# Prompt attention in a hybrid decoder layer: 64-row score tiles without key padding, scores two units ahead, softmax division on GpSimd

## What is computed

```python
A_HEADS = 16; A_KV = 4; A_HD = 64; A_GROUP = 4; WINDOW = 128; SEQ = 1024

def sink_attend(q, k, v, mask, sinks):
    s = jnp.einsum('...kgqd,...ksd->...kgqs', q, k).astype(f32) * (A_HD ** -0.5)
    s = jnp.where(mask, s, -jnp.inf)
    sk = sinks.astype(f32)[:, :, None]
    mx = jnp.maximum(jnp.max(s, axis=-1), sk)
    p = jnp.exp(s - mx[..., None])
    den = jnp.sum(p, axis=-1) + jnp.exp(sk - mx)
    return jnp.einsum('...kgqs,...ksd->...kgqd', (p / den[..., None]).astype(v.dtype), v)

def swa_prompt(q, k, v, sinks):
    # blocks of 128 queries read their own block of keys and the previous one
    ...
    mask = (diff >= 0) & (diff < WINDOW) & (kpos[:, None, :] >= 0)
    o = sink_attend(qb, band(k), band(v), mask[:, None, None], sinks)
```

## Time and profile before

| what | us |
|---|---|
| median of 3 runs | 1845.52 (1844.2 to 1847.49) |
| span of the profiled execution | 1838.2 |
| of it first half of the prompt attention | 549 to 677 |
| sampled tokens | 677 to 782 |
| second half of the prompt attention | 782 to 899 |
| busy in the whole span: PE | 1774.4 (97%) |
| DVE | 809.4 (44%) |
| ACT | 523.1 (28%) |
| POOL | 72.4 (4%) |

### The profile page before, as it was taken

One profiled execution on the slowest core, in us unless ns is written; L12 is line 12 of the kernel. 1 busy time (PEld: TensorE's weight loads), 2 busy tenths in 40 slices (PEclk: granted clock), 3 DMA queues, 4 the chain that ended last, 5 costly groups with the idle time before them and its releaser, 6 DMA issues.

```text
span 1838.2 us, 26328 instructions
## 1 busy us (share of the span) xinstructions
PE 1774.4 (97%) x10443; PEld 1622.1 (88%) x10443; DVE 809.4 (44%) x1769; ACT 523.1 (28%) x1191; POOL 72.4 (4%) x149
## 2 busy tenths in 40 slices
PE   7999977998999999999999999999999999999998
PEld 7999956996899888888999998888888889999996
DVE  5313212342115544466452544444444544444447
ACT  5424311331224533345330331211121222222222
POOL 3001110110100000000000100000000000000001
PEclk9999986998899999999999999999999999999999
DMA  6131125212512112311133011111111111111112
GB/s 199 48 90 43 45 60 94 41 35 73 72 29 41 24 32 50 67 24 24 24 93 109 24 47 47 46 46 46 46 46 40 30 44 46 46 46 46 46 58 97
DMA packets 140605, 99.26 MB, mean 54 GB/s; under 512 B 82328, under 2 KB 132512, under 8 KB 140520
## 3 DMA queue, kind: packets, MB, share of 16 engines
q1 hardware_dynamic: 140520, 98.08, 20.6%
HBM read 88.43 MB, written 11.60 MB: 54 GB/s over the span
## 4 chain that ended last, share of the span: by engine, by line
PE 85%; DMA 5%; SPq 1%; DVE 1%; ACT 0%; issue 0%; POOL 0%; POOLq 0%; ACTq 0%; DVEq 0%
PE bank L725 25%; PE bank L1077 21%; PE bank L1050 21%; PE bank L1036 6%; DMA out<-Cin 4%; PE bank L865 3%; PE bank L687 3%; PE bank L897 2%; PE bank L782 1%; PE bank L790 1%; PE bank L808 1%; PE bank L819 1%; PE bank L785 1%; DMA bc<-gate_rows 1%; DMA Cin<-in_state_n 0%; PE bank L765 0%
## 5 line engine op out<-in xcount | busy, mean ns | idle before, releaser
L1891 DVE TENSOR_TENSOR x<-bank,x 128x512 f32<-128x512 f32 x288 | 195.5, 689 | 139.2 <-PE bank L1077 137.5
L1050 PE MATMUL bank<-xT_hi,w_hi 128*128 128x384 f32 (+1 forms) x768 | 250.5, 326 | 1.0 <-DVE xT_lo L1513 1.0
L1050 PE MATMUL bank<-xT_hi,w_lo 128*128 128x384 f32 (+1 forms) x768 | 250.4, 326 | 0.0
L1050 PE MATMUL bank<-xT_lo,w_hi 128*128 128x384 f32 (+1 forms) x768 | 250.3, 326 | 0.0
L1077 PE MATMUL bank<-w_hi,hid_hi 128*128 128x512 f32 x576 | 227.1, 394 | 0.0
L1077 PE MATMUL bank<-w_lo,hid_hi 128*128 128x512 f32 x576 | 226.1, 392 | 0.0
L1077 PE MATMUL bank<-w_hi,hid_lo 128*128 128x512 f32 x512 | 204.1, 399 | 0.0
L725 PE MATMUL bank<-xT_hi,w_hi 128*128 128x384 f32 (+1 forms) x1008 | 197.7, 338 | 3.5 <-ACT w_hi L1124 3.5
L725 PE MATMUL bank<-xT_lo,w_hi 128*128 128x384 f32 (+1 forms) x1008 | 189.6, 330 | 0.0
L725 PE MATMUL bank<-xT_hi,w_lo 128*128 128x384 f32 (+1 forms) x1008 | 186.5, 326 | 0.0
L1448 ACT ACTIVATE relu<-bank 128x384 f32<-128x384 f32 (+1 forms) x96 | 45.4, 473 | 493.8 <-PE bank L1050 493.8
(11 more groups left out here) (204 smaller groups left out, 2330.8 us busy)
## 6 DMA issues: line engine op xcount, KB each, us to landing
raw<-in_w_in SPq DMA_DIRECT2D x64, 256.0 KB, 4.4
raw<-in_w_up SPq DMA_DIRECT2D x16, 1024.0 KB, 5.5
raw<-in_w_down SPq DMA_DIRECT2D x16, 1024.0 KB, 4.9
raw<-in_w_in SPq DMA_DIRECT2D x10, 1024.0 KB, 5.9
xin<-in_x_prompt SPq DMA_DIRECT2D x8, 512.0 KB, 4.0
Cin<-in_state_C SPq DMA_DIRECT2D x8, 512.0 KB, 4.4
bc<-gate_rows SPq DMA_DIRECT2D x32, 128.0 KB, 4.2
out<-Cin SPq DMA_DIRECT2D x8, 512.0 KB, 6.2
```

The source lines that it names most:

```text
L1050: last = nc.tensor.matmul(bank[n % 4][:, 0:cn], w[:, slot, k * WCOLS + tile * P:k * WCOLS + (tile + 1) * P], x[:, k, c0:c0 + cn], start=(s ...
L1891: nc.vector.tensor_tensor(v, bank[4 + d % 4][:, :], v, ALU.add).then_inc(free_v, 1)
```

## The change

Four things change together, all in the prompt attention.

First, the keys are kept without padding in `akT`, two heads in 128 rows. A score matmul takes 64 rows, rows 0 to 63 or 64 to 127, and they alternate; the two halves write different banks. To make that possible a unit is now a block with two query heads of each of two key heads (`gg`). ACT writes `akT` with one copy instead of two, GpSimd no longer clears `akz`, and the keys are transposed for the output with 4 transposes instead of 8 float32 matmuls. The value matmuls take columns from both units of the pair and run key block by key block.

Second, PE makes scores two units ahead: S(0) and S(1) before the first fill, S(n+2) in slot n. S(n+2) still waits for the mask of n+1, since banks 3 and 4 are as before. `prob` and `ast` have three buffers. ACT's order in a slot stays as it was.

Third, in the last slot of a half the transposes come before the fill.

Fourth, the division moves from DVE to GpSimd, with a power of -1 in place of the reciprocal.

```diff
-            akz = a("akz", [P, NKV, T])
+            akT = a("akT", [P, 2, T])
...
-                prob = a2("prob", [P, 2, GRP, 2 * P])
+                prob = a2("prob", [P, 3, GRP, 2 * P])
                 pT = a2("pT", [P, 2, 2, GRP * P])
-                ast = a2("ast", [P, 2, 6, GRP])
+                ast = a2("ast", [P, 3, 6, GRP])
...
             def at_scores(u):
-                i, p, half = at_unit(u)
-                kv = 2 * p + half
+                i, p, gg = at_unit(u)
                 lo = 0 if i else P
                 if u >= 1:
                     pe.wait_ge(at_m, u)
-                for g in range(GRP):
-                    out = bank[3 + g // 2][:, (g % 2) * 256 + lo:(g % 2) * 256 + 256]
-                    last = nc.tensor.matmul(out, aqT[:, p * GRP + g, cols(i)],
-                                            akz[:, kv, (i - 1) * P + lo:(i + 1) * P], start=True, stop=True)
+                for g in range(2):
+                    for half in range(2):
+                        at = slice(64 * half, 64 * half + 64)
+                        out = bank[3 + half][:, g * 256 + lo:g * 256 + 256]
+                        last = nc.tensor.matmul(out, aqT[at, p * GRP + 2 * gg + g, cols(i)],
+                                                akT[at, p, (i - 1) * P + lo:(i + 1) * P], start=True, stop=True)
                 last.then_inc(at_s, 1)
 
...
-                        last = tr(bank[5 + kb][:, g * P:(g + 1) * P], prob[:, u % 2, g, kb * P:(kb + 1) * P], P)
+                        last = tr(bank[5 + kb][:, g * P:(g + 1) * P], prob[:, u % 3, g, kb * P:(kb + 1) * P], P)
...
                     pe.wait_ge(at_o, pair)
-                for half in range(2):
-                    u, kv = 2 * pair + half, 2 * p + half
-                    for kb in range(2):
-                        if kb:
-                            pe.wait_ge(at_p1, u + 1)
-                        elif i:
-                            pe.wait_ge(at_p0, prev_count(u))
-                        if kb or i:
-                            last = nc.tensor.matmul(bank[7][64 * half:64 * half + 64, :],
-                                                    avn[:, i - 1 + kb, kv * HD:(kv + 1) * HD], pT[:, half, kb, :],
+                u = 2 * pair + 1
+                for kb in range(2):
+                    if kb:
+                        pe.wait_ge(at_p1, u + 1)
+                    elif i:
+                        pe.wait_ge(at_p0, prev_count(u))
+                    if kb or i:
+                        for half in range(2):
+                            kv = 2 * p + half
+                            out = bank[7][64 * half:64 * half + 64, :].rearrange("d (a c) -> d a c", a=2)
+                            last = nc.tensor.matmul(out, avn[:, i - 1 + kb, kv * HD:(kv + 1) * HD],
+                                                    pT[:, :, kb, 256 * half:256 * half + 256],
                                                     start=(kb == 0 or i == 0), stop=(kb == 1))
                 last.then_inc(at_v, 1)
...
                 at_scores(u0)
+                at_scores(u0 + 1)
                 fill(fills[0])
                 for n in range(HALF):
                     u = u0 + n
-                    if n + 1 < HALF:
-                        at_scores(u + 1)
-                        at_transposes(u)
-                        fill(fills[n + 1])
-                    else:
-                        fill(fills[n + 1])
-                        at_transposes(u)
+                    if n + 2 < HALF:
+                        at_scores(u + 2)
+                    at_transposes(u)
+                    fill(fills[n + 1])
                     if n % 2:
                         at_values(u // 2)
...
                 for x, i in enumerate((NT - 2, NT - 1)):
-                    for kv in range(NKV):
-                        p, half = divmod(kv, 2)
-                        last = nc.tensor.matmul(bank[5 + x][0:rows_of(i), p * P:(p + 1) * P], akz[:, kv, cols(i)],
-                                                ident[:, :], start=(half == 0), stop=(half == 1))
+                    for p in range(2):
+                        last = tr(bank[5 + x][0:rows_of(i), p * P:(p + 1) * P], akT[:, p, cols(i)], P)
                     last.then_inc(ko_t, 1)
...
-                    for half in range(2):
-                        at = slice(64 * half, 64 * half + 64)
-                        ins = nc.scalar.activation(akz[at, 2 * tile + half, c0:c0 + cn], src[at, 0:cn], ACT.Copy)
-                    ins.then_inc(free_a, 1)
+                    nc.scalar.activation(akT[:, tile, c0:c0 + cn], src[:, 0:cn], ACT.Copy).then_inc(free_a, 1)
...
+                    at_prev(u)
                     if n + 1 < HALF:
-                        at_prev(u)
                         at_exps(u + 1)
-                        fill(fills[n + 1])
-                    else:
-                        fill(fills[n + 1])
-                        at_prev(u)
+                    fill(fills[n + 1])
                     if n % 2:
                         at_out(u // 2)
...
-                if u >= 2:
-                    dve.wait_ge(at_t, u - 1)
-                st = ast[:, u % 2]
+                if u >= 3:
+                    dve.wait_ge(at_t, u - 2)
+                st = ast[:, u % 3]
...
-                sk = sink_b[:, kv * GRP:(kv + 1) * GRP]
-                link(nc.vector.scalar_tensor_tensor(st[:, 1, :], st[:, 0, :], ATT_SCALE, sk, ALU.mult, ALU.max))
+                sk = sink_b[:, :].rearrange("t (v g) -> t v g", g=GRP)[:, 2 * p:2 * p + 2, 2 * gg:2 * gg + 2]
+
+                def by_half(x):
+                    return st[:, x, :].rearrange("t (v g) -> t v g", g=2)
+                link(nc.vector.scalar_tensor_tensor(by_half(1), by_half(0), ATT_SCALE, sk, ALU.mult, ALU.max))
                 nc.vector.tensor_scalar(st[:, 2, :], st[:, 1, :], -1.0, None, ALU.mult)
-                nc.vector.tensor_tensor(st[:, 3, :], sk, st[:, 1, :], ALU.subtract).then_inc(at_m, 1)
-
-            def at_divide(u):
-                lo = 0 if at_unit(u)[0] else P
-                dve.wait_ge(at_e, u + 1)
-                st = ast[:, u % 2]
-                link(nc.vector.tensor_tensor(st[:, 5, :], st[:, 4, :], st[:, 3, :], ALU.add))
-                link(nc.vector.reciprocal(st[:, 5, :], st[:, 5, :]))
-                for g in range(GRP):
-                    v = prob[:, u % 2, g, lo:]
-                    ins = nc.vector.tensor_scalar(v, v, st[:, 5, g:g + 1], None, ALU.mult)
-                ins.then_inc(at_p, 1)
+                nc.vector.tensor_tensor(by_half(3), sk, by_half(1), ALU.subtract).then_inc(at_m, 1)
 
...
                 at_mask(u0)
-                at_divide(u0)
+                at_mask(u0 + 1)
                 fill(fills[0])
                 for n in range(HALF):
                     u = u0 + n
-                    if n + 1 < HALF:
-                        at_mask(u + 1)
-                        at_own(u)
-                        at_divide(u + 1)
-                        fill(fills[n + 1])
-                    else:
-                        fill(fills[n + 1])
-                        at_own(u)
+                    if n + 2 < HALF:
+                        at_mask(u + 2)
+                    at_own(u)
+                    fill(fills[n + 1])
 
...
-            for kv in range(NKV):
-                link(nc.gpsimd.memset(akz[64 * (1 - kv % 2):64 * (1 - kv % 2) + 64, kv, :], 0.0))
             link(nc.gpsimd.memset(amask[:, :], 0.0))
             keep_where(amask[:, 0:P], [[1, P]], -1, -1, ALU.is_ge, -BIG).then_inc(consts, 1)
             keep_where(amask[:, P:2 * P], [[-1, P]], 0, 1, ALU.is_ge, -BIG).then_inc(consts, 1)
+
+            def at_divide(u):
+                lo = 0 if at_unit(u)[0] else P
+                pool.wait_ge(at_e, u + 1)
+                st = ast[:, u % 3]
+                link(nc.gpsimd.tensor_tensor(st[:, 5, :], st[:, 4, :], st[:, 3, :], ALU.add))
+                link(nc.gpsimd.tensor_tensor(st[:, 5, :], st[:, 5, :], negone[:, :], ALU.pow))
+                for g in range(GRP):
+                    v = prob[:, u % 3, g, lo:]
+                    ins = nc.gpsimd.tensor_scalar(v, v, st[:, 5, g:g + 1], None, ALU.mult)
+                ins.then_inc(at_p, 1)
+
+            for u in range(2 * HALF):
+                at_divide(u)
```

More of the change, by code:

```diff
@@ L920, in ss_scores @@
                     nc.tensor.matmul(out[:, 0:P], q, kcT[at, b % 2, p, :], start=True, stop=True)
-                    last = nc.tensor.matmul(out[:, P:192], q, akz[at, kv, SEQ:T], start=True, stop=True)
+                    last = nc.tensor.matmul(out[:, P:192], q, akT[at, p, SEQ:T], start=True, stop=True)
                 last.then_inc(ss_s, 1)
@@ L1293, in at_exps @@
                 act.wait_ge(at_m, u + 1)
-                nc.scalar.activation(ast[:, u % 2, 3, :], ast[:, u % 2, 3, :], ACT.Exp)
+                nc.scalar.activation(ast[:, u % 3, 3, :], ast[:, u % 3, 3, :], ACT.Exp)
                 for g in range(GRP):
```

(15 more changed lines are left out.)

5 lines of the change are left out of this document (3 added, 2 removed).

## The result

The changed kernel takes 1901.36 us (1896.5 to 1906.2), against 1844.92 for the kernel before on the same chip: a ratio of 1.0298, 95% interval [1.0277, 1.0319]. The profiled execution has a span of 1894.8 (before 1838.2) and took 1896.48 us, so a run's time is 1.7 us over its span; the rest of the 7 us between span and median, here as before, is that the profiled execution was shorter than the median. Forecast were 1859.5 and a range of 1840 to 1874: the sign was right, the size was not.

What follows compares the result with a forecast made beforehand. PE bound the kernel before; afterwards the loop would bound even slots, PE odd ones. Waits of 10.7 against 9.0 gained per half, less key transposes, gave +1.7; the port 12.5: 14 us on 1845.5, so 1859.5, range 1840 to 1874.

Steps and rivals of the forecast that it cites:

- The loop's formula: Prompt attention, last transposes of one unit to first of the next: 3.20 + D = 6.25 us, bounding even slots only.
- the term D: GpSimd's division of one unit: sum 0.31, power 1.06, four products 1.68, together 3.05 us, bounds 2.65 and 4.4.
- The clock (e): Rival: PE's clock falls behind its waits of 1 to 3 us in the attention halves; called small, no chance given.
- The port: GpSimd's products and DVE's two-input SBUF operations exclude each other in the attention: 12.5 us in sum, bounds 0 and 18.
- gates: DVE operations of 0.55 and 0.56 us, second half, meeting GpSimd's products: 1.05 in each of 6 even slots.
- weight rests: DVE subtractions, halves of 1.2 us, near the end of GpSimd's products in 6 even slots, hitting perhaps a third: 2.5 us.
- PE's work: Prompt attention: row tiles save 13.0, shape changes cost 4.7, last values gain 0.7; PE's work falls 9.0 us per half.
- Rival (d): Row tiles of the score matmuls don't overlap, so PE gains nothing: 1873 us; chance 0.07.
- start wait of 1.7: At the start of each half S(1) waits for the mask of unit 0, which nothing covers: 1.7 us.
- key transposes: Key transposes for the output, 16 instructions in 2.11 us, become 4 of the 0.11 kind, once: 1.7 us saved.
- Rival (c): GpSimd's product costs like a two-input one, 0.65 us: D = 4.0, odd slots begin to wait, 1877 us; chance 0.11.

## Why the prediction was wrong

**The loop's formula was right, the term D in it was not.** The step that failed is the price of GpSimd's four products, 0.42 us each with 0.75 as the upper bound; they took 0.91 each. The forecast had the loop at 3.20 + D from the last transpose; measured are 602.12 - 593.98 = 8.14 with D = 5.04, so 3.10 + D, and slope 1 over four sizes. D was 3.05, with bounds 2.65 and 4.4, and came out at 5.04, outside both. Of its parts the sum was 0.31 (0.28), the power 1.06 (1.13 with its gap), the products 4 x 0.42 = 1.68 (3.63). The upper bound was 0.75, the two-input product of the earlier trace rows, on the belief that one input can't cost more than two; on GpSimd it does. The value 0.42 rested on a memset and a selection in the earlier trace rows, which do no arithmetic on fp32 columns. The Trainium skill, "GPSIMD Engine Reference", 3.1, has a best case of 769 ns for 512 elements, 1.5 ns each; here it is 2.5 ns and 0.2 us besides. Even its price, dearer than mine, was too low. (DVE, for comparison, took 0.35 for the same product.)

With D = 5.04 the forecast's own working gives per half: even slots 6 x (8.24 - 5.2) = 18.2, odd ones from 3 to 11, now bound as well, 5 x (8.24 - 7.07) = 5.9, slot 13 2.4, slot 14 4.3, start 1.7: 32.5 in place of 10.7. For both halves this is 43.6 more. That odd slots are bound by the loop too follows from D; the forecast had them free.

**The clock (e) was dismissed.** I called it small because it was 1.00 before; but before, PE never waited in these halves. The halves of the changed kernel are 6.0 and 3.6 longer than those with PE kept busy, 9.6 in all, and somewhat more, since that run had 2 us more of long products. The length of a wait does not decide alone whether it falls. In the changed kernel it fell behind 13 of the 15 waits of 2.6 to 4.8 us: behind eleven the transposes took 1.57 to 1.98, behind two only the fill was slower. Behind a wait of 3.48 and one of 2.88 it stayed; the transposes behind the first:

```profile
932.12 1.11 PE bank L688 x8
```

In the run with one product by a constant it fell behind four of eight waits of 1.75 to 1.78 us, one of them here, and not behind one of 2.42:

```profile
593.41 1.92 PE bank L688 x8
595.33 4.96 PE bank L726 x24
```

With the broadcast product it stayed behind a wait of 1.91 and fell behind one of 1.89. What decides is open.

**The port was there, and oversized.** In the changed kernel 20 of the 112 products of 256 columns are more than 50 ns over the 922 of the others, by 7.6 us in sum (2.7 and 4.9 in the halves), for instance this one of 1.72 us, the second of three that start at 580.58, beside a DVE subtraction of two SBUF tensors:

```profile
580.58 3.52 POOL L2043 TENSOR_SCALAR prob<-prob,ast 128x256 f32<-128x256 f32 x3
...
581.18 1.23 DVE L1482 TENSOR_TENSOR w_lo<-raw,w_hi 128x1024 fp32r<-128x1024 f32 x1 [3.62 <-ACT w_hi L1124]
```

Forecast were 12.5, 10.0 of it for gates and 2.5 for weight rests. But seven products beside the weight rests (L1482) took 1.63 to 1.90 and make 6.0 of the 7.6; beside gates a product took 0.98 to 1.23, 1.6 in sum. The meeting was foreseen, but 1.05 for a slot with two gates was too high by far and the price of the rests too low, so that the sum is off by less than its parts. The Trainium skill, "SBUF — State Buffer", Who interferes with whom, says that the two exclude each other; the trace agrees with 1.72 against 0.92.

**PE's work was right.** Forecast -9.0 per half, measured -9.3 and -9.2 (division on DVE), with scores at 1.06 for eight. Rival (d) is out. The start wait of 1.7 is 1.5 here, for the mask, in each half:

```profile
552.14 0.71 PE L867 MATMUL bank<-akT,aqT 64*128 64x128 f32 x8 [1.49 <-DVE ast L1676]
```

The key transposes went from 2.11 to 0.4, the 1.7 that were forecast.

**MLP's 6.9** was in no term: a change of 16 bytes in the layout was not read as a change at all.

The miss is 1901.4 - 1859.5 = 41.9. Its parts: D +43.6, clock +9.6 (to 11.6), port 7.6 - 12.5 = -4.9, MLP -6.9, between attention and MLP +1.3, PE's work and the start waits -0.9: 41.8 to 43.8, up to 2 more than the miss. The agreement is partly luck: the first part comes from the forecast's formula and not from a measurement, and with the measured 3.10 in it instead of 3.20 it is 2.6 smaller, 0.1 in each of 26 slots. Rival (c) named the right term, at D = 4.0 and 1877, and stopped a microsecond short.

## What to carry to other kernels

Price an engine by a row of the same operation on the same engine, or bound it far above; a dearer form on paper (two inputs) is no upper bound there. Before an engine is put into a loop, ask what the loop waits for: here swapping two calls on ACT, or one broadcast product for four, took back nearly the whole loss, and leaving the division where it was turned 1.030 into 0.986. A wait on TensorE costs itself, and often a slow stretch behind it: here behind 13 of the 15 waits of 2.6 us and more, and behind some of 1.8.

## What the runs showed of the hardware

- GpSimd's fp32 product with one tensor and a scalar takes about 0.2 us and 2.5 ns a column (851 ns for 256, 2.8 us for 1024), 70 ns more with a scalar per partition; a product of two tensors, one of them broadcast, took 1.90 for 1024.
- Matmuls on two 64-row tiles in fp32 overlap: eight of 256 columns in 1.06 us, 1.73 on whole rows. The transposes behind them take 0.04 to 0.05 more each time, and a half's fills 1.1 more (73.2 to 74.3).
- Sixteen bytes more a partition, allocated ahead of MLP's tensors, made the 512-column matmuls there 1% faster, 6.9 us in all; sixty bytes did not.
- Behind 11 of 15 waits of 2.6 to 4.8 us PE ran eight transposes in 1.57 to 1.98 us instead of 1.04, at a granted clock of 0.50 to 0.69, and matmuls that nobody reads, put in the gap, cured nearly all of it. The same came behind waits of 1.75 to 1.78 us in four of eight cases, and stayed away behind two of 3.48 and 2.88.
